# Latent attention in a two-block kernel: absorbed key and value projections, stacked rope queries, split probabilities, two query tiles per product

## The reference

```python
q  = cq @ w_qup_h          # 128 plain columns, 64 rope columns (rotated)
k, v = split(ckv @ w_kvup_h)           # 128 and 128 columns
s  = (q_plain @ k.T + rotate(q_rope) @ kp.T) / sqrt(192)
o  = softmax(s) @ v
y_h = o * silu(gate_h)
```

## Time and profile before

| | us |
|---|---|
| median of 3 runs | 2891.39 (2888.91 to 2892.69) |
| profiled execution, first to last instruction | 2889.4 |
| PE busy | 2729.1 (94% of the span) |
| DVE, ACT, POOL busy | 1252.2, 636.4, 644.7 |
| the heads, first product to last gating | 1850.5 to 2397.2 |

### The profile page before, as it was taken

The page is one execution under the profiler, slowest core; times in us unless marked ns, Lnnn a source line. Parts: engine busy times, 40 slices in busy tenths (PEclk is TensorE's granted clock), DMA queues, the critical chain, the costliest instruction groups (busy, mean ns, idle before and its releaser), DMA issues.

```text
span 2889.4 us, 34178 instructions
## 1 busy us (share of the span) xinstructions
PE 2729.1 (94%) x13082; PEld 2208.3 (76%) x13082; DVE 1252.2 (43%) x1521; ACT 636.4 (22%) x850; POOL 644.7 (22%) x360
## 2 busy tenths in 40 slices
PE   7978888999999899999999989999999999899997
PEld 4756666777877688888888868788888887677776
DVE  5644334764133533144224563355555554522243
ACT  3133332010111321011001232233333332211120
POOL 2200111333332223333233322200000002222231
...
DMA packets 40418, 143.59 MB, mean 50 GB/s; under 512 B 4972, under 2 KB 6252, under 8 KB 39950
## 3 DMA queue, kind: packets, MB, share of 16 engines
...
...
## 4 chain that ended last, share of the span: by engine, by line
PE 80%; DVE 10%; issue 5%; ACT 3%; DMA 2%; DVEq 0%; ACTq 0%; SPq 0%
PE PS L421 58%; PE PS L784 5%; PE PS L746 3%; PE PS L749 3%; PE PS L762 2%; DMA AW<-in_ada 2%; PE PS L462 1%; PE PS L843 1%; PE PS L839 1%; PE PS L434 1%; PE PS L454 1%; DVE H L1314 1%; ACT SA L958 1%; DVE SA L1442 1%; DVE SA L1426 1%
## 5 line engine op out<-in xcount | busy, mean ns | idle before, releaser
L421 PE MATMUL PS<-H,w_hl 128*128 128x512 f32 x6624 | 1550.9, 395 | 64.1 <-DVE H L1314 16.3
L421 PEld LDWEIGHTS PS<-H,w_hl 128*128 128x128 f32 x6624 | 1255.0, 190 | 351.1 <-issue 47.0
L396 POOL CAST w_hl<-w_raw 128x1024 fp32r<-128x1024 f32 x176 | 188.1, 1069 | 2171.8 <-PE PS L421 2171.8
L398 POOL TENSOR_TENSOR w_hl<-w_raw,w_hl 128x1024 fp32r<-128x1024 f32 x176 | 447.4, 2542 | 14.1
L421 PE MATMUL PS<-FF,w_hl 128*128 128x512 f32 x1056 | 239.8, 389 | 0.0
L421 PEld LDWEIGHTS PS<-FF,w_hl 128*128 128x128 f32 x1056 | 198.3, 188 | 41.1
L784 PE MATMUL PS<-PT,VN 128*128 128x128 f32 x1280 | 153.6, 275 | 0.4 <-DVE PT L1752 0.3
L784 PEld LDWEIGHTS PS<-PT,VN 128*128 128x128 f32 x1280 | 147.9, 192 | 0.9 <-DVE PT L1752 0.9
L746 PE MATMUL PS<-KN,QN 128*128 128x512 f32 (+1 forms) x576 | 146.8, 363 | 0.5 <-DVE QP L1728 0.5
L749 PE MATMUL PS<-KPE,QP 128*128 128x512 f32 (+1 forms) x576 | 142.3, 355 | 0.0
L1738 DVE TENSOR_REDUCE cols<-PS 128x1 f32<-128x1280 f32 x64 | 95.4, 1491 | 99.2 <-PE PS L749 99.2
...
## 6 DMA issues: line engine op xcount, KB each, us to landing
...
```

Source lines behind the costliest of these rows:

```text
L396: pool.tensor_copy(hi_part, raw).then_inc(w_hi, 1)
L398: pool.tensor_tensor(lo_part, raw, hi_part.bitcast(F32), ALU.subtract).then_inc(w_split, 1)
L421: mm = pe.matmul(PS[:, out_at + a:out_at + a + m], w(s, wp, w0 + k), src[:, o:o + m], start=(k == 0 and wp == 0 and xp == 0), stop=(k == k ...
```

## The change

The key projection is applied to the query weights instead of the keys, and the value projection after the weighted sum instead of before: `absorb` makes AH, the product of the head's plain query weights and key weights (6 matmuls of 128 columns), `queries` makes queries in latent space QN = AH.T cq, and scores are taken against CKV itself. CKT, CKV transposed once, stands for the values; `weighted_values` multiplies it with the probabilities of two query tiles at a time (256 columns), now split into high and low parts in three float32r passes, and `values` applies the value weights to 512 queries at once. Rope queries are rotated and summed on DVE into 64 rows, whose high part lies on partitions 0 to 63 and low part on 64 to 127 of QPS, so two passes against KPE do. The normalisation moves to ACT, but for tile 1 of each head. Waits and semaphores follow. Only the host's layout of the weight units changes beside it.

The diff, added lines; the removed functions are those printed above, "..." marks what is left out.

```diff
@@ tiles
...
+QPS = at("QPS", T, H_AT + 8192, F32R)
+KPE = at("KPE", 2 * TK, H_AT + 12288, F32R)
+CKT = at("CKT", 2 * TK, H_AT + 22528, F32R)
+E = at("E", 2 * TK, H_AT + 32768)
+PT = at("PT", 2 * PTW, H_AT + 43008, F32R)
+AH = at("AH", 2 * 256, H_AT + 63488, F32R)
+OL = at("OL", 2 * HALF, T_AT, F32R)
+OLF = at("OLF", HALF, F_AT + 59392)
+ROT = [TMP0, SQ]
...
@@ helpers
...
+def block_cols(part, t, k0, k1):
+    o = part * PTW + k0 * GQ
+    return PT[:, o:o + (k1 - k0) * GQ].rearrange("p (k c) -> p k c", c=GQ)[:, :, (t % 2) * P:(t % 2 + 1) * P]
+def bank_cols(bank, k0, k1):
+    return PS[:, bank:bank + (k1 - k0) * P].rearrange("p (k c) -> p k c", c=P)
@@ tensor
...
+def absorb(h, hh, opens=False):
...
+    for c in range(2):
+        for n, (wp, xp) in enumerate(PASSES):
+            mm = pe.matmul(PS[:, 3072 + c * P:3072 + (c + 1) * P], w(s, wp, c), w(s, xp, 2),
+                           start=(n == 0), stop=(n == 2))
+            if opens and c == 0 and n == 0:
+                mm.then_inc(w_used, 1)
+    mm.then_inc(hp_done, 1)
+def rope_queries(h, hh):
+    s = (hu + hh) % 2
+    feature_major(s, CQ, 2 * T, T, 2, 0, w0=3, opens=False).then_inc(hp_done, 1)
+def queries(h):
+    pe.wait_ge(ah_lo, h + 1)
+    for c in range(2):
+        for ap, xp in PASSES:
+            for a in (0, 512):
+                o = xp * 2 * T + c * T + a
+                mm = pe.matmul(PS[:, 1536 + a:2048 + a], AH[:, ap * 256 + c * P:ap * 256 + (c + 1) * P],
+                               CQ[:, o:o + 512], start=(c == 0 and ap == 0 and xp == 0),
+                               stop=(c == 1 and ap == 1))
+    mm.then_inc(hp_done, 1)
+PIECES = ((0, 512), (512, 512), (1024, 256))
+def nope_scores(t, a, m, ends=False):
+    base = 1536 * (t % 2)
+    for n, (qp_, kp_) in enumerate(PASSES):
+        mm = pe.matmul(PS[:, base + a:base + a + m], QN[:, qp_ * T + t * P:qp_ * T + (t + 1) * P],
+                       CKV[:, kp_ * TK + a:kp_ * TK + a + m], start=(n == 0), stop=False)
+        if ends and n == 0:
+            mm.then_inc(w_used, 1)
+def rope_scores(t, a, m):
+    base = 1536 * (t % 2)
+    for kp_ in range(2):
+        mm = pe.matmul(PS[:, base + a:base + a + m], QPS[:, t * P:(t + 1) * P],
+                       KPE[:, kp_ * TK + a:kp_ * TK + a + m], start=False, stop=(kp_ == 1))
+    return mm
+def mla_scores(h, t, ends=False):
+    for a, m in PIECES:
+        if a == 1024 and t >= 2:
+            pe.wait_ge(pt_lo, (h * 8 + (t - 2)) * 3 + 2)
+        nope_scores(t, a, m, ends and a == 0)
+        mm = rope_scores(t, a, m)
+    mm.then_inc(sc_done, 1)
+def first_scores(h):
+    pe.wait_ge(qn_lo, h + 1)
+    for a, m in PIECES:
+        nope_scores(0, a, m)
+    pe.wait_ge(qp_lo, h + 1)
+    for a, m in PIECES:
+        mm = rope_scores(0, a, m)
+    mm.then_inc(sc_done, 1)
+def transpose_blocks(t, k0, k1, bank):
+    for kb in range(k0, k1):
+        mm = pe.transpose(PS[:, bank + (kb - k0) * P:bank + (kb - k0 + 1) * P],
+                          E[:, (t % 2) * TK + kb * P:(t % 2) * TK + (kb + 1) * P], ident[:, :])
+    mm.then_inc(tp_done, 1)
+def transposes(h, t, last):
+    tg = h * 8 + t
+    pe.wait_ge(e_ready, tg + 1)
+    if t == 0:
+        pe.wait_ge(o_gated, h * 2 + 1)
+    elif t == 4 and not last:
+        pe.wait_ge(ah_lo, h + 2)
+    elif t == 6:
+        pe.wait_ge(o_gated, h * 2 + 2)
+    elif t % 2:
+        pe.wait_ge(pt_lo, (tg - 1) * 3 + 1)
+    transpose_blocks(t, 0, 4, 3072)
+    transpose_blocks(t, 8, 10, 1280 + 1536 * (t % 2))
+    if t % 2:
+        pe.wait_ge(pt_lo, (tg - 1) * 3 + 3)
+    else:
+        pe.wait_ge(ol_copied, h * 4 + (t // 2 + 1))
+    transpose_blocks(t, 4, 8, 3584)
+def weighted_values(h, g):
+    pe.wait_ge(pt_lo, (h * 8 + (2 * g + 1)) * 3 + 3)
+    for kb in range(10):
+        for vp, xp in PASSES:
+            mm = pe.matmul(PS[:, 3584:3584 + GQ], CKT[:, vp * TK + kb * P:vp * TK + (kb + 1) * P],
+                           PT[:, xp * PTW + kb * GQ:xp * PTW + (kb + 1) * GQ],
+                           start=(kb == 0 and vp == 0 and xp == 0), stop=(kb == 9 and vp == 1))
+    mm.then_inc(pv_done, 1)
+def values(h, hh, j):
+    s = (hu + hh) % 2
+    pe.wait_ge(ol_lo, h * 4 + (2 * j + 2))
...
+        mm = pe.matmul(PS[:, 3072:3584], w(s, wp, 5), OL[:, xp * HALF:(xp + 1) * HALF],
...
+    mm.then_inc(op_done, 1)
...
+    for g in range(4):
+        t = 2 * g
+        transposes(h, t, last)
+        if g < 3:
+            mla_scores(h, t + 2)
...
+            rope_queries(h + 1, 1 - hh)
+        transposes(h, t + 1, last)
+        if g < 3:
+            mla_scores(h, t + 3)
+        elif not last:
+            queries(h + 1)
+        if g == 1 and not last:
+            pe.wait_ge(pt_lo, (h * 8 + 3) * 3 + 1)
+            absorb(h + 1, 1 - hh)
+        if g == 2:
+            pe.wait_ge(pt_lo, (h * 8 + 5) * 3 + 1)
+            values(h, hh, 0)
+        weighted_values(h, g)
...
+        values(h, hh, 1)
+        mla_scores(h + 1, 1, ends=True)
+    else:
+        values(h, hh, 1)
...
+absorb(0, 0, opens=True)
+for part in range(2):
+    for kb in range(10):
+        mm = pe.transpose(PS[:, 1536 * part + kb * P:1536 * part + (kb + 1) * P],
+                          CKV[:, part * TK + kb * P:part * TK + (kb + 1) * P].bitcast(F32), ident[:, :])
+    mm.then_inc(ct_done, 1)
+pe.wait_ge(ct_hi, 1)
+rope_queries(0, 0)
+pe.wait_ge(ct_lo, 1)
+queries(0)
...
+mla_scores(0, 1)
...
+pe.wait_ge(o_gated, 2 * HEADS + 1)
...
@@ scalar
...
+def absorbed_hi(h):
+    act.wait_ge(hp_done, h * 3 + 1)
+    act.activation(AH[:, 0:256], PS[:, 3072:3328], ACT.Copy).then_inc(ah_hi, 1)
+def queries_hi(h):
+    act.wait_ge(hp_done, h * 3 + 3)
+    act.activation(QN[:, 0:T], PS[:, 1536:2560], ACT.Copy).then_inc(qn_hi, 1)
+def rope_hi(h):
+    act.wait_ge(qp_sum, h + 1)
+    act.activation(QPS[0:64, :], TMP0[0:64, :], ACT.Copy).then_inc(qp_hi, 1)
...
+    act.wait_ge(mx_ready, h * 8 + (t + 1))
...
+def normalise(h, t):
+    act.wait_ge(rc_ready, h * 8 + (t + 1))
+    act.wait_ge(ex_ready, h * 8 + (t + 1))
+    e = E[:, (t % 2) * TK:(t % 2) * TK + TK]
+    act.activation(e, e, ACT.Copy, scale=cols[:, 24 + t % 2:25 + t % 2]).then_inc(e_ready, 1)
+def probs_hi(h, t):
+    for n, (k0, k1, bank) in enumerate(((0, 4, 3072), (8, 10, 1280 + 1536 * (t % 2)), (4, 8, 3584))):
+        act.wait_ge(tp_done, (h * 8 + t) * 3 + (n + 1))
+        act.activation(block_cols(0, t, k0, k1), bank_cols(bank, k0, k1), ACT.Copy).then_inc(pt_hi, 1)
+def latent_hi(h, g):
+    act.wait_ge(ol_copied, h * 4 + (g + 2))
+    if g % 2 == 0:
+        act.wait_ge(op_done, h * 2 + (g // 2 + 1))
+    o = (g % 2) * GQ
+    act.activation(OL[:, o:o + GQ], OLF[:, o:o + GQ], ACT.Copy).then_inc(ol_hi, 1)
+def mla_head(h, last=False):
+    for g in range(4):
+        t = 2 * g
+        probs_hi(h, t)
+        if g == 0:
+            mla_exp(h, 1)
+        probs_hi(h, t + 1)
+        if g < 3:
...
+            normalise(h, t + 2)
+            mla_exp(h, t + 3)
+            normalise(h, t + 3)
+        elif not last:
+            queries_hi(h + 1)
+            rope_hi(h + 1)
+        if g == 1 and not last:
+            absorbed_hi(h + 1)
+        latent_hi(h, g)
...
+        mla_exp(h + 1, 0)
+        normalise(h + 1, 0)
+absorbed_hi(0)
+act.wait_ge(ct_done, 1)
+act.activation(CKT[:, 0:TK], PS[:, 0:TK], ACT.Copy).then_inc(ct_hi, 1)
+rope_hi(0)
+queries_hi(0)
+mla_exp(0, 0)
+normalise(0, 0)
...
+        mla_head(i * 2 + hh)
+mla_head(HEADS - 2)
+mla_head(HEADS - 1, last=True)
+act.wait_ge(o_gated, 2 * HEADS + 1)
...
@@ vector
...
+def absorbed_lo(h):
+    v.wait_ge(ah_hi, h + 1)
+    v.tensor_tensor(AH[:, 256:512], PS[:, 3072:3328], AH[:, 0:256].bitcast(F32), ALU.subtract).then_inc(ah_lo, 1)
+def queries_lo(h):
+    v.wait_ge(qn_hi, h + 1)
+    v.tensor_tensor(QN[:, T:2 * T], PS[:, 1536:2560], QN[:, 0:T].bitcast(F32), ALU.subtract).then_inc(qn_lo, 1)
...
+    v.wait_ge(hp_done, h * 3 + 2)
+    for n in range(2):
+        rows = slice(64 * n, 64 * n + 64)
+        v.tensor_tensor(ROT[n][0:64, :], PS[rows, 0:T], CSQ[rows, :], ALU.mult).then_inc(rot_done, 1)
+def rotated(h):
+    v.wait_ge(rot_done, h * 2 + 2)
+    v.tensor_tensor(TMP0[0:64, :], ROT[0][0:64, :], ROT[1][0:64, :], ALU.add).then_inc(qp_sum, 1)
+def rope_lo(h):
+    v.wait_ge(qp_sum, h + 1)
+    v.wait_ge(qp_hi, h + 1)
+    v.tensor_tensor(QPS[64:128, :], TMP0[0:64, :], QPS[0:64, :].bitcast(F32), ALU.subtract).then_inc(qp_lo, 1)
...
+    v.wait_ge(sc_done, h * 8 + (t + 1))
...
+def inverse(h, t):
+    v.wait_ge(ex_ready, h * 8 + (t + 1))
+    v.reciprocal(cols[:, 24 + t % 2:25 + t % 2], cols[:, 18 + t % 2:19 + t % 2]).then_inc(rc_ready, 1)
+def second_tile(h):
+    v.wait_ge(rc_ready, h * 8 + 2)
+    e = E[:, TK:2 * TK]
+    v.tensor_scalar(e, e, cols[:, 25:26], None, ALU.mult).then_inc(e_ready, 1)
+def probs_lo(h, t):
+    for n, (k0, k1, bank) in enumerate(((0, 4, 3072), (8, 10, 1280 + 1536 * (t % 2)), (4, 8, 3584))):
+        v.wait_ge(pt_hi, (h * 8 + t) * 3 + (n + 1))
```

(66 more changed lines are left out.)

165 lines of the change are left out of this document (14 added, 151 removed).

## The result

The changed kernel has a median of 2825.97 us (2823.84 to 2828.65, 4 runs) against 2891.76 (2888.91 to 2892.69): ratio 0.9777, interval 0.9763 to 0.9791, so 65.8 us less. The forecast was 2830, range 2808 to 2857.

The account below looks back on a forecast made before the run. PE's own instruction stream was taken to bound the heads: 53.7 us of slots plus 5.0 of waits gave a 58.7 us period; with the ends, 61.6 us less, span 2827.8, median about 2830, range 2808 to 2857.

Parts of the forecast that it names:

- Slots: PE's matmul start-to-start distances in each head: sum falls from 64.9 to 53.7 us, 11.2 less; 256-column passes at 0.120.
- Tile 4: PE's wait of 1.5 us before these transposes, for the absorbed weights' low part, its high-part copy queued on ScalarE.
- Group 3's products: PE's wait of 0.8 us before these weighted values, with rotation standing on VectorE ahead of the probabilities' low parts.
- Tile 0: PE's wait of 1.3 us, was 0.96, in the next head: maximum, exp, reciprocal and normalisation take 4.9, covered for 3.6.
- Tile 1: PE's wait of 0.9 us in the next head: exp queued behind three high-part copies, then normalisation on VectorE.
- Tile 6: PE's wait of 0.2 us for gating, queued behind a reciprocal.
- Rival 2: Engines behind PE slower than priced, strided PT at 1.3 times: about 2.5 us more per head, 2850 us; chance 0.08.
- The start: Work ahead of head 0's first transposes: these come at about 1872.3, 1.5 us later than 1870.83.
- The end: Last head: 36.7 us to the end of group 2's products, then 12.7 to the last gating; 3 us allowed for clock.
- Rival 1: The clock falls once in each head, adding 1.7 to 3.4 us each: 2844 to 2857 us; chance 0.17.
- Rival 3: PE's waits in the heads are half those walked, 2.5 x 8 = 20 us less: 2810 us; chance 0.10.
- The rule on order: PE waits where needed work is queued behind other work on ScalarE or VectorE, as 1.5 us at tile 4.

Follow-up runs that it names:

- the filled start: Changed kernel with 18 and 8 unread 512-column products filling PE's two waits in head 0: one run, 2828.24 us; first product to first transposes 22.58 us for 24.01.

## Why the prediction was right

It gave 2830 for 2826, a period of 58.7 for 58.28, and the mechanism was the one found: PE's slots set the time, and what is not won of them is waits, three of them from the order of queues and tile 0's at the end of a chain. Point by point:

- **Slots.** 256-column products with a new weight each: 30 from 1882.09 to 1885.69, 0.120. Score passes and transposes kept their slots (10 transposes in 1.0 to 1.1 us with their wait). The period of head 1 is 58.28, so 4.6 us are left beside the 53.7 of slots: 4.1 stand at four places, and the other 0.4 has no place in the row of its own.
- **Waits.** The forecast's waits are distances between slots, so they are set against the same measure (above), not against the brackets. Tile 4: 1.5 foretold, 1.49 measured, on AH. Group 3's products: 0.8, 0.61. Tile 0: 1.3, 1.48, on E from ScalarE. Tile 1: 0.9, 0.57, on E from VectorE. Tile 6: 0.2, but 0.40 in head 0 and 0 to 0.14 in the others. The two that the walk had too long hang on three copies in a row. It added up whole durations, 0.59 + 0.38 + 0.59 on ScalarE and 0.68 + 0.41 + 0.68 on VectorE, but the rows show 1.36 and 1.62 for three:

```profile
1932.78 1.36 ACT L1249 ACTIVATE PT<-PS 128x512 fp32r<-128x512 f32 x3 [0.82 <-PE PS L800]
...
1933.40 1.62 DVE L1866 TENSOR_TENSOR PT<-PS,PT 128x512 fp32r<-128x512 f32 x3 [0.52 <-ACT PT L1249]
```

  That is 0.2 and 0.15 less. With VectorE's normalisation at 0.89 for the 0.94 of the forecast it is about the size of both misses. Tile 0's wait was 0.2 longer than foretold; ScalarE's normalisation accounts for 0.03 of that, and the rest stays open. The five waits named in the forecast add up to 4.7 (the other 0.3 of its 5.0 was for small ones inside the pairs), and measured they are 4.1 in head 1. So the total was 0.6 us too long, and misses of both signs cancel in it. The small ones did not show: tile 2's transposes start at 1885.69, at the end of the 30 slots from 1882.09.
- **Normalisation** took 1.364 us, I had 1.33 from exp's row. The 1.36 that I worked out with the Trainium skill (ScalarE: Activation LUTs, What ACT_TABLE_LOAD costs: about 93 ns for a per-partition pointer operand) agrees with it.
- **Strided destinations** cost nothing: 598 ns for ScalarE's 512 columns against 589 contiguous, 686 on VectorE against my 0.68. Rival 2 is out.
- **The start** came out at 1872.44 for 1872.3 by luck: the heads began 2.05 us earlier by chance, and the stretch was 3.66 us longer instead of 1.5. Of these 2.16 us more, the clock accounts for 1.43, which the filled start gave back by the first transposes; it was at half after PE's idle 4.3 us (PEclk 0.54). Where the other 0.7 lies stays open. **The end** was 50.0 us for 49.4 + 3 allowed for the clock. Filling PE's waits there gave back 1.5 us, so the allowance was mis-sized by half. Of the 4.1 us that the span lies under the forecast of 2827.8, 2.4 are this end, 1.4 the seven periods and 0.5 what comes after, less 0.1 at the start.
- **Rival 1** (the clock falls in each head) didn't happen: 1.00 over all looped heads. It was near, though. The same kernel with shorter products, or with a wait of 1.9 to 2.5 us at tile 0, had it. Rival 3 had the waits at half, 2.5 us; they were 4.6 in all (58.28 - 53.7), against the 5.0 forecast, so it is out.
- **The rule on order** held when turned round, for two waits: tile 4's gave 1.4 of its 1.49 when the copy was moved, and group 3's 0.54 of its 0.61 when one rotation product was. Tile 6's was hardly there outside head 0. Tile 0's wait, which ends a chain, shrank from 1.32 to 0.84 with a step 0.48 shorter. Tile 1's, put down to the order of ScalarE's queue, stayed at 0.3 to 0.4 (bracket) wherever the scores were no longer and the clock was at 1.00, and no run changed that order.

What is argued and not shown is the worth of absorbing the projections by itself. It stands on the slots alone: 39 products fewer per head, most of 128 columns, and 12 more, about 3 us of the 11.2 of slots. No run undid it.
